# A fused transformer block: a partial sum carried from bank to bank, norms behind roundings, eight weight units loaded early, a maximum taken as a minimum

## The reference

```python
# window attention, a block of 128 queries against up to 384 keys
s = jnp.where(valid, s, -jnp.inf)
m = jnp.maximum(jnp.max(s, axis=-1, keepdims=True), sk)
p = jnp.exp(s - m)
p = p / (jnp.sum(p, axis=-1, keepdims=True) + jnp.exp(sk - m))
...
# retention, the end
yn = ((y - mu) * lax.rsqrt(var + EPS)).reshape(B, S, RET_WIDTH) * gn_w
return silu(g) * yn
...
mix = jnp.concatenate([a, r], axis=-1) @ w_out[l]        # 1024x1024 @ 1024x1024: "O"
x = x + rms_norm(mix, norm_mix_post[l])                  # "post" rows
h = rms_norm(x, norm_xa_pre[l])                          # "pre" rows
mn = rms_norm(mem, norm_mem[l])
q = (h @ xa_wq[l]).reshape(B, S, XA_HEADS, XA_HEAD_DIM)
kv = (mn @ xa_wkv[l]).reshape(B, M, 2, XA_HEADS, XA_HEAD_DIM)   # 256x1024 @ 1024x2048
```

## Time and profile before

| what | value |
| --- | --- |
| median of three runs | 1409.26 us (1408.86 to 1410.67) |
| the profiled execution | 1407.63 us, of which 1405.7 are the span of the trace |
| granted TensorE clock | full over the whole span |
| PE busy | 98% of the span |
| DVE, ACT, POOL busy | 63%, 47%, 62% |
| DMA | 183.59 MB, mean 131 GB/s |

### The profile page before, as it was taken

How to read it: one execution, slowest core, us unless ns; L and a number is a source line. 1 busy time by engine, 2 the same in 40 slices (tenths; PEclk the granted TensorE clock), 3 DMA queues, 4 the chain that set the end, 5 groups by cost and what they waited for, 6 DMA issues and landing times.

```text
span 1405.7 us, 18988 instructions
## 1 busy us (share of the span) xinstructions
PE 1377.9 (98%) x6708; PEld 1144.0 (81%) x6708; DVE 883.8 (63%) x1286; ACT 663.3 (47%) x1345; POOL 871.9 (62%) x602
## 2 busy tenths in 40 slices
PE   8999999999999999999999999999999999999998
PEld 7998888756978778888888888888888888888886
DVE  5799997887958977855267633333333333375868
ACT  6432233666675765354365533333333333544455
POOL 1597256422777866611354687777777774699653
PEclk9999999999999999999999999999999999999999
DMA  5676133530027374310536133333333324933354
GB/s 202 203 248 212 46 91 104 177 124 1 1 68 269 113 250 148 90 52 24 187 97 218 39 112 112 113 113 98 109 100 107 113 83 152 364 121 91 109 210 153
DMA packets 137758, 183.59 MB, mean 131 GB/s; under 512 B 10304, under 2 KB 82368, under 8 KB 137664
## 3 DMA queue, kind: packets, MB, share of 16 engines
q1 hardware_dynamic: 135360, 177.25, 38.5%
q10 hardware_dynamic: 2304, 5.13, 1.0%
HBM read 136.98 MB, written 45.35 MB: 130 GB/s over the span
## 4 chain that ended last, share of the span: by engine, by line
PE 81%; DVE 10%; POOL 4%; ACT 3%; issue 2%; DMA 0%; DVEq 0%; POOLq 0%; ACTq 0%
PE ps L1306 24%; PE ps L1308 24%; PE ps L1307 24%; PE ps L1302 4%; PE ps L1803 2%; DVE x L3266 1%; PE ps L1480 1%; DVE y L3262 1%; DVE sm L3059 1%; PE ps L1518 1%; PE ps L1572 1%; DVE y L3272 1%; DVE x L3672 1%; POOL ws L1220 1%; DVE yf L3665 1%
## 5 line engine op out<-in xcount | busy, mean ns | idle before, releaser
L1306 PE MATMUL ps<-w_hi,t_hi 128*128 128x512 f32 (+2 forms) x576 | 220.7, 383 | 5.5 <-POOL w_lo L1109 3.5
L1307 PE MATMUL ps<-w_lo,t_hi 128*128 128x512 f32 (+2 forms) x576 | 218.3, 379 | 0.0
L1308 PE MATMUL ps<-w_hi,t_lo 128*128 128x512 f32 (+2 forms) x576 | 218.3, 379 | 0.0
L1066 POOL TENSOR_TENSOR w_lo<-raw,w_hi 128x512 fp32r<-128x512 f32 (+1 forms) x52 | 81.7, 1577 | 97.7 <-ACT w_hi L2082 97.6
L1306 PEld LDWEIGHTS ps<-w_hi,t_hi 128*128 128x128 f32 x576 | 108.9, 189 | 25.5 <-POOL w_lo L1109 5.1
L1308 PEld LDWEIGHTS ps<-w_hi,t_lo 128*128 128x128 f32 x576 | 108.9, 189 | 17.8
L1307 PEld LDWEIGHTS ps<-w_lo,t_hi 128*128 128x128 f32 x576 | 108.9, 189 | 17.0
L1190 POOL TENSOR_TENSOR w_lo<-raw,w_hi 128x512 fp32r<-128x512 f32 x32 | 41.7, 1319 | 98.2 <-ACT w_hi L2520 98.2
L3565 DVE TENSOR_TENSOR ev<-ps,ev 128x512 f32<-128x512 f32 x21 | 14.5, 692 | 138.2 <-PE ps L1308 138.2
L2719 ACT ACTIVATE ev<-ps 128x512 f32<-128x512 f32 x63 | 37.5, 595 | 83.8 <-PE ps L1308 83.8
L2082 ACT ACTIVATE w_hi<-raw 128x512 fp32r<-128x512 f32 (+1 forms) x52 | 31.4, 616 | 96.6 <-PE ps L1308 96.1
(11 more groups left out here) (386 smaller groups left out, 4138.1 us busy)
## 6 DMA issues: line engine op xcount, KB each, us to landing
raw_a<-in_ffn_w_gu_dram SPq DMA_DIRECT2D x44, 256.0 KB, 3.3
raw_b<-in_ffn_w_gu_dram SPq DMA_DIRECT2D x44, 256.0 KB, 3.2
f_rows<-fs SPq DMA_DIRECT2D x44, 256.0 KB, 3.8
gain_b<-f_rows SPq DMA_DIRECT2D x39, 256.0 KB, 2.7
tables<-f_rows SPq DMA_DIRECT2D x38, 256.0 KB, 2.7
f_rows<-fa SPq DMA_DIRECT2D x33, 256.0 KB, 3.5
raw<-in_xa_wkv_dram SPq DMA_DIRECT2D x32, 256.0 KB, 3.2
raw<-in_xa_wo_dram SPq DMA_DIRECT2D x32, 256.0 KB, 2.6
```

Source lines behind the costliest of these rows:

```text
L1066: nc.gpsimd.tensor_tensor(w_lo[:, k, 0:width], raw[:, k, 0:width], w_hi[:, k, 0:width].bitcast(F32), ALU.subtract).then_inc(w_split, 1)
L1306: nc.tensor.matmul(out, a_hi, b_hi, start=start, stop=False, skip_group_check=onto)
L1307: nc.tensor.matmul(out, a_hi, b_lo, start=False, stop=False, skip_group_check=onto)
L1308: return nc.tensor.matmul(out, a_lo, b_hi, start=False, stop=stop, skip_group_check=onto)
```

## The change

It has four parts.

1. **Attention.** The reduction multiplies by -scale, starts from `nsink` (one column a head) and takes the minimum, so it gives `wnm` directly; the instruction at L3063 goes, and the exponentials wait for each head's reduction.
2. **Order at O's start.** ACT's roundings of units 5 to 11 stand ahead of more of the norms, POOL's low parts ahead of more mixes; DVE norms two heads of all eight row tiles (16 instructions, before 12), ACT the other two.
3. **Carried sums.** S1 accumulates onto product 11: ACT copies product 11's result from bank 4+m to bank m (`o_carry(1, m)`) before S1's first matmul there. Product 12 does so onto `part` (`o_carry(6, m)`). DVE's joins of S4 and 12 and POOL's two additions of parts go; four ACT copies each take S4's and 12's results to `y` (`o_kept`).
4. **First key/value units.** Units 0 to 3 are loaded straight into `t_lo_f`, the place of their low parts, behind x's first rows on SP's queue, and 4 to 7 behind unit 27. ACT rounds 0 to 3 between the roundings of units 16, 17 and 18, POOL makes their low parts between those of 16, 17 and 18. On ACT the rounding of unit 20 stands ahead of the memory rows' square roots.

The diff, cut to its core:

```diff
@@ SP @@
-            out_loads(RING, 17)
+            def first_kv(a):
+                sp.wait_ge(w_used, U_O + (5 if a else 3) * RING)
+                for n in range(a, a + RING):
+                    c, k = divmod(n, NK)
+                    kk, cols = kv_home(n)
+                    sp.dma_start(t_lo_f[:, kk, cols], wkv_v[k, :, c * 512:(c + 1) * 512]).then_inc(kv_in[a // RING], 16)
+            out_loads(RING, 18)
             sp.wait_ge(turned, TURNED["mem"])
             x_back(0, 3, 5)
-            out_loads(17, 20)
+            first_kv(0)
+            out_loads(18, 20)
...
             out_loads(24, 7 * RING)
+            first_kv(RING)
@@ POOL @@
-            def first_and_fifth(h):
-                pool.wait_ge(part_out, 8)
-                p = part[:, 2 * h:2 * h + 2, :]
-                nc.gpsimd.tensor_tensor(p, p, part[:, 4 + 2 * h:6 + 2 * h, :], ALU.add).then_inc(o_p5, 1)
+            def first_kv_low(k):
+                kk, c = kv_home(k)
+                pool.wait_ge(w_rounded, U_O + RING + k + 1)
+                low = nc.gpsimd.tensor_tensor(t_lo[:, kk, c], t_lo_f[:, kk, c], t_hi[:, kk, c].bitcast(F32), ALU.subtract)
+                if k == NK - 1:
+                    low.then_inc(w_split, NK)
@@ PE: what frees the banks, and who starts a sum @@
                 elif kind == "S1":
                     pe.wait_ge(dve_ev, lows + 4)
-                    pe.wait_ge(o_raw, O_RAW + 4 + m + 1)
+                    pe.wait_ge(o_carried, O_CARRIED + m + 1)
...
                 elif kind == "12":
-                    pe.wait_ge(o_joined, m + 1)
-                    pe.wait_ge(dve_ev, DVE_EV["mem"] + m + 1)
+                    pe.wait_ge(o_carried, O_CARRIED + 4 + m + 1)
...
-                first = kind in ("11", "S1", "S2")
+                first = kind in ("11", "S2")
@@ ACT @@
+            def o_carry(j, m):
+                if j == 1:
+                    o_tile_ready(0, m)
+                    act.wait_ge(o_raw, O_RAW + 4 + m + 1)
+                    src = bank(4 + m)
+                else:
+                    act.wait_ge(dve_ev, DVE_EV["mem"] + m + 1)
+                    src = part[:, 4 + m, :]
+                nc.scalar.activation(bank(m), src, ACT.Copy).then_inc(o_carried, 1)
+            def first_units(*units):
+                for k in units:
+                    kk, c = kv_home(k)
+                    act.wait_ge(kv_in[k // RING], KV_IN[k // RING] + 64)
+                    nc.scalar.activation(t_hi[:, kk, c], t_lo_f[:, kk, c], ACT.Copy).then_inc(w_rounded, 1)
...
             round_out(25)
+            for m in range(4):
+                o_carry(6, m)
             sums(("pre", 0), ("post", 2))
             round_out(26)
-            first_units(0)
             round_out(27)
-            sums(("pre", 1))
-            first_units(1)
-            sums(("post", 3))
+            first_units(4, 5)
+            sums(("pre", 1), ("post", 3))
+            first_units(6, 7)
+            o_kept(6, 0)
@@ DVE @@
-                                                   1.0, -3.0e38, ALU.add, ALU.max, wmx[:, n, h:h + 1]).then_inc(w_max, 1)
+                                                   -A_SCALE, nsink[:, h:h + 1], ALU.add, ALU.min,
+                                                   wnm[:, n, h:h + 1]).then_inc(w_max, 1)
                 dve.wait_ge(w_max, G * (s + 1))
                 hs = slice(g * G, (g + 1) * G)
-                nc.vector.scalar_tensor_tensor(out=wnm[:, n, hs], in0=wmx[:, n, hs], scalar=-A_SCALE, in1=nsink[:, hs],
-                                               op0=ALU.mult, op1=ALU.min).then_inc(w_small, 1)
...
-            for m in range(4):
-                o_join(2, m)
...
-            o_join(6, 0)
-            o_join(6, 1)
             post_rows(3)
-            o_join(6, 2)
```

More of the change, by code:

```diff
@@ L1155, in _ @@
             third_sum(1)
-            low_parts(13, 15)
-            first_and_fifth(0)
-            low_part(15)
-            first_and_fifth(1)
-            low_parts(16, 7 * RING)
+            low_parts(13, 17)
+            first_kv_low(0)
+            first_kv_low(1)
+            low_part(17)
+            first_kv_low(2)
+            first_kv_low(3)
+            low_parts(18, 28)
+            for k in range(4, NK):
+                first_kv_low(k)
             def mem_low(n):
@@ L2341, in _ @@
                 act.dma_start(mem_rows(m), mem[0, m * P:(m + 1) * P, :]).then_inc(mem_in, 16)
-            for k in range(16, 20):
-                round_out(k)
+            round_out(16)
+            first_units(0, 1)
+            round_out(17)
+            first_units(2, 3)
+            round_out(18)
+            round_out(19)
             o_sum_high(2, 0)
             o_sum_high(2, 1)
+            round_out(20)
             for m in range(NM):
@@ L2348, in _ @@
                             lambda: act.wait_ge(mem_in, 32))
-            for k in range(20, 24):
-                round_out(k)
+                round_out(21 + m)
+            round_out(23)
             rounds = 0
@@ L2385, in mem_high @@
                                          bank(2 * m + half).rearrange("p (k i) -> p k i", k=4), ACT.Copy).then_inc(m_act, 1)
-            def first_units(*units):
-                for k in units:
-                    kk, c = kv_home(k)
-                    act.wait_ge(w_loaded[k % RING], 16 * ((U_KV + k) // RING))
-                    act.wait_ge(w_used, U_O + (3 if k < RING else 5) * RING)
-                    nc.scalar.activation(t_hi[:, kk, c], raw[:, k % RING, :], ACT.Copy).then_inc(w_rounded, 1)
             sums(("post", 0), ("post", 1))
@@ L2401, in _ @@
             round_out(25)
+            for m in range(4):
+                o_carry(6, m)
             sums(("pre", 0), ("post", 2))
             round_out(26)
[L2404 removed]
             round_out(27)
[L2406 to L2417 removed]
+            first_units(4, 5)
+            sums(("pre", 1), ("post", 3))
+            first_units(6, 7)
+            o_kept(6, 0)
+            sums(("post", 4), ("pre", 2))
+            o_kept(6, 1)
+            sums(("post", 5), ("pre", 3))
+            o_kept(6, 2)
             sums(("post", 6), ("pre", 4))
+            o_kept(6, 3)
             round_units(RING)
@@ L2440, in _ @@
                 if c == 0:
[L2441 removed]
+                    act.wait_ge(o_joined, 12)
                 for t in range(NM):
```

147 lines of the change are left out of this document (73 added, 74 removed).

## The result

The changed kernel takes 1412.46 us (median of 12 runs, 1411.40 to 1415.00) where 12 runs of the kernel before gave 1409.16: a ratio of 1.0025, 95% interval 1.0014 to 1.0035. It is slower, by 3.5 us by the ratio (the medians lie 3.3 apart). The time lies in the range of the prediction, but the change was forecast to win 0.4 us, and it loses more than the measurement's uncertainty.

The account below looks back on a forecast made before the run. PE was taken to bound the kernel (busy 98%, 81% of the chain), DVE holding some stages. Attention -1.4, DVE's chain -2.7 and S3's end +3.7 sum to -0.4: from a 1409.26 median to 1408.8 us, range 1402.0 to 1413.5.

Parts of the forecast that it names:

- Start of O: At the start of the O projection, PE's waits for late low parts go: -4.0 us.
- The new wait for unit 17: In S3, PE waits for unit 17's low part, held behind the fourth key/value load landing at 437.7: +6.5 us.
- Unit 18 ... 3 x 1.3 = 3.9 against the 2.7 us of a unit: +1.2: In S3, POOL makes two key/value low parts ahead of unit 18's, so PE waits again: +1.2 us.
- Four joins of the last product leave it: ... -2.5: On DVE's chain to the key/value product, four joins of 0.62 us each go: -2.5 us.
- The hole of +1.9: Before pre row 0, DVE idles because ACT's four carries stand ahead of that row's square root: +1.9 us.
- The four low parts that leave the rows, -2.1: From 471.5 to 480, DVE's row operations shorten because POOL no longer makes four key/value low parts there: about -2.1 us.
- The sign that was named for it: In the profile after, DVE's row operations in 470 to 480 would take 1.3 us.
- Attention, -1.4: In attention, one DVE instruction less a step shortens the chain by 0.20 us in seven blocks: -1.4 us.
- rival C: In attention, reductions starting from a column take 0.06 us longer: +1.7, so 1410.5 us; chance 0.05.
- the end of S3: Start of O's -4.0 and the waits for units 17 and 18, +7.7, put S3's end at +3.7 us.
- -2.7: DVE's chain to the key/value product: joins -2.5, hole +1.9, quieter row operations about -2.1; together -2.7 us.
- Rival B: In S3, key/value loads land at 440.8, low parts beside DVE take 1.8 us each: +5.0, 1414.3 us; chance 0.22.

Follow-up runs that it names:

- e2: Changed kernel with only ACT's loads of the gain and two memory rows moved behind the rounding of unit 17; ratio 1.0010 to the kernel before.
- e11: e8 with product 12 added up as in the kernel before: four joins on DVE, no carries or copies for it; ratio 0.9988 to the kernel before.
- e8: Changed kernel without its fourth part (early key/value units), with two of product 12's four carries moved behind the roots; ratio 0.9982 to the kernel before.
- e4: Changed kernel with the roundings of units 26 and 27 ahead of the square roots of pre row 0 and post row 2; ratio 1.0025 to the kernel before.
- e9: Changed kernel, transfers unmoved, with unit 17 ahead of the first key/value units on ACT and POOL, and unit 18's low part ahead of theirs; ratio 1.0032.
- e7: Changed kernel without its fourth part (early key/value units), all four carries still ahead of the roots; ratio 1.0001 to the kernel before.
- e1: Changed kernel with the first four key/value units later: loads behind those of units 18 and 19, roundings behind units 20 and 21; ratio 1.0001.
- e6: Changed kernel with early key/value loads behind units 18 and 19, rounded ahead of unit 20, low parts spread out, carries split; 1406.17 us, ratio 0.9974.

## Why the prediction was wrong

- **Start of O: right.** Unit 8 starts 25.4 us after O's first matmul instead of 29.4, 4.0 less, and POOL's or the carry's waits there are nil. The four copies from bank to bank took 2.10 together, 0.53 each, a little over the 0.51 that was taken for them, and PE didn't wait for them. But 0.8 of the 4.0 is lost again at unit 13, whose low part comes late out of POOL's backlog (424.08).
- **The new wait for unit 17: right in place and mechanism.** Forecast: the fourth unit lands at 437.7, unit 17 is ready at 442.2, 6.5 late. Measured: 436.5, 441.0 and 5.9, in an execution in which O starts 1.5 us earlier. That the landing fits so well is partly luck. ACT's queue issued gain and memory rows from 422.20 on, 3.6 us before the forecast: ahead of the four copies that stand before them in the program (423.84), so these delayed nothing. SP's load of unit 17 went later than forecast, at 424.05 instead of 423.5. From 429.96 on the ten pieces up to the fourth unit took 0.66 us each, not 0.80. The pieces landed in the order of their issue over both queues, as the prediction took it, but e2, which moved six of them away, gained only 1.2 us.
- **What followed that wait: the first step that failed.** "Unit 18 ... 3 x 1.3 = 3.9 against the 2.7 us of a unit: +1.2". It priced POOL's low parts as if DVE were quiet. DVE was busy beside them, and the three took 5.7 us, so unit 18 came 3.0 us late and not 1.2. The clock was low meanwhile, and no term for it stood in the sum, but at this place it cost nothing: e2 has it back in time and the same 5.66 us. With the 0.8 of unit 13 and small differences, the start of product 22, relative to O's first matmul, came 5.9 us later than before and not 3.7.
- **"Four joins of the last product leave it: ... -2.5": the second step that failed.** It took DVE's operations as a sum of fixed lengths. e11 puts the joins back and loses 0.8 us by the ratios, less than their uncertainty, with stages within 0.3; the stage from pre row 0 to the query product is 73.3 in e8 with four joins less and 73.2 in the kernel before. What the joins give, 2.7 us, the row operations take, 2.1 us, because more of them then lie beside POOL. This is shown without the early units; in the changed kernel the two changes work together.
- **What PE does behind S3: left out.** The sum went by DVE's chain alone. PE's waits in the last product, 0.3 us before and 3.6 in the changed kernel, with low clock behind them, had no term: O's last product takes 16.2 us from its first matmul to its last instead of 11.2. What DVE wins behind pre row 0 can only shorten PE's waits in the key/value product, and these fell from 4.0 to 1.7. DVE gets from pre row 0 to pre row 4 in 27.6 us instead of 32.3, about as much less as the joins and the early low parts were forecast to give together (4.6), but the query product comes only 2.4 earlier. How much of the 5.0 us of the last product is on the changed kernel's path is open (e4).
- **The hole of +1.9: right** (2.14 idle on DVE), and splitting the carries gives 0.8 to 1.4 us in the changed kernel, 2.7 without the early units.
- **The four low parts that leave the rows, -2.1: right in size**; from pre row 0 to the query product the changed kernel takes 70.8 us, e8 without the early units 73.3. The sign that was named for it did not come: in 470 to 480 three of the row operations still take 2.13 to 2.20 us (472.29, 474.60, 476.76), beside the low parts of units 4 to 7, which POOL makes from 470.87 on.
- **Attention, -1.4: right in size, wrong in reason.** 0.20 us less a block is not there; with reductions 0.06 longer (rival C's mechanism, given 0.05) the quiet blocks are slower by 0.3 us in four. The gain seems to be in the blocks beside POOL.

With the end of S3 at +5.9 instead of +3.7 and -0.2 instead of -2.7 behind it, the sum of 1408.8 becomes 1413.5, and the measured time is 1412.5. Rival B, the slower one, at 1414.3 and 0.22, had the right side and part of the right mechanism: low parts at 1.8 each beside DVE, and unit 18 2.0 us late. Its condition, a landing at 440.5, did not come.

## What to carry to other kernels

Work that is pulled ahead must not stand in front of a unit with a due time on any in-order queue: here one wait on a semaphore for four transfers held ACT, then POOL, then PE, although unit 17's own load had landed at 430. Where two engines hold each other up, as DVE's row operations and POOL's low parts do, an operation taken off one of them isn't won: ask what the other will then stand beside. A wait of PE can cost more than its length when the clock falls with it, unless the next operand is later still, as unit 18's was. And a loss can lie behind a loss: taking away the wait of S3 gave about a third of what it moved product 22.

## What was not expected of the hardware

- The granted clock fell to half, 1.2 GHz, around single idle stretches of PE, and the length of the stretch alone doesn't tell when. Behind 5.75 us (441.04) it was low at once, and 12 matmuls ran 0.43 apart. In e9 waits of 2.50 and 1.70 us were followed by a whole unit at full speed, while in e7 one of 2.22 us (517.02) was followed by a matmul of 0.79. In e1 a wait of 2.67 us (453.20) was followed by three matmuls at full speed and then, from 454.36 on, by slow ones, 0.43 apart. In the changed kernel 2.31 was followed by full speed, and 1.25 right behind it by the low level. e6, whose waits in O are all under 1.3 us, has none. The Trainium skill (TensorE: Matmul & The Clock Gate, Part 1: The HAM clock gate) tells of two levels, 1.2 and 2.4 GHz, between which PE's activity decides; the rows agree.
- DVE's operations between SBUF tiles and POOL's hold each other up in both directions: 1.23 against 2.19 us for an addition (e1), 1.27 against 2.25 for a low part (after, 439.72 and 444.41). Joins, which read a bank, do not: low parts beside them take 1.3 us (e8, e11). Four DVE instructions of 0.16 us took 1.03 to 1.25 in attention before.
- ACT's queue issued three DMAs up to 1.6 us before four copies that stand ahead of them in the program had begun (after, 422.20 against 423.84).
- With only SP's queue issuing, the same transfers ran slower than with both, 340 against 377 to 399 GB/s (one profile, e2). No run here says why.
